# Giving each weight load of the front to the ring slot whose chunk the plan uses up first

## The reference

```
mod = silu(c) @ w_ada + b_ada                      # 2048 x 12288: shift, scale, gate, twice
h = rmsnorm(x, g_mix) * (1 + sc1) + sh1
proj = h @ w_in                                    # 2048 x 5136, columns split among three heads:
#   A: Mamba-2 SSD (conv, silu, chunked scan)   B: HGRN2 (gated recurrence)   C: S5 (diagonal scan)
x = x + gt1 * (concat(out_a, out_b, out_c) @ w_out)
h = rmsnorm(x, g_ffn) * (1 + sc2) + sh2
x = x + gt2 * hmoe(h)                              # 32 experts of width 256, top 2 inside the top group
y = rmsnorm(x, g_final)                            # and the new states are returned
```

## Time and profile before

| | |
|---|---|
| median of 3 runs | 1537.83 us (1534.4 to 1539.6) |
| the profiled execution | 1539.11 us |
| its span in the profile | 1537.4 us |
| granted TensorE clock, mean | 0.889 of 2.4 GHz |
| TensorE matmul busy | 1242.3 us (81%) |
| VectorE busy | 516.8 us (34%) |
| ScalarE busy | 197.2 us (13%) |
| GpSimd busy | 269.1 us (18%) |
| DMA | 387.06 MB, mean 252 GB/s |

### The profile page before, as it was taken

The page is one execution under the profiler, slowest core; times in us unless marked ns, Lnnn a source line. Parts: engine busy times, 40 slices in busy tenths (PEclk is TensorE's granted clock), DMA queues, the critical chain, the costliest instruction groups (busy, mean ns, idle before and its releaser), DMA issues.

```text
span 1537.4 us, 14850 instructions
## 1 busy us (share of the span) xinstructions
PE 1242.3 (81%) x5948; PEld 683.2 (44%) x5948; DVE 516.8 (34%) x1014; ACT 197.2 (13%) x319; POOL 269.1 (18%) x580
## 2 busy tenths in 40 slices
PE   5899999998979797989979785877888786878625
PEld 2456556454546464656557472332333332333214
DVE  2412657544752862245531331211112111111044
ACT  1311111101201310231210220000000000000011
POOL 3170388870000000021120002010000010000010
PEclk9899999999998898889989866999899998899856
DMA  9998468765663636352122503999999999999441
GB/s 343 363 364 299 166 216 277 268 225 177 215 222 110 219 110 219 125 150 84 55 69 110 218 31 103 421 421 419 413 413 404 404 394 413 400 412 409 203 137 69
DMA packets 140342, 387.06 MB, mean 252 GB/s; under 512 B 15435, under 2 KB 54757, under 8 KB 112814
## 3 DMA queue, kind: packets, MB, share of 16 engines
q1 hardware_dynamic: 132208, 361.91, 62.4%
q0 software_dynamic: 6784, 18.76, 3.5%
q10 hardware_dynamic: 1280, 5.42, 1.0%
HBM read 385.97 MB, written 23.15 MB: 266 GB/s over the span
## 4 chain that ended last, share of the span: by engine, by line
PE 47%; DMA 26%; DVE 10%; POOL 10%; issue 3%; ACT 2%; SPq 1%; DVEq 0%; POOLq 0%; ACTq 0%
DMA slot<-in_w_exp_up 20%; PE psum L1402 10%; PE psum L1069 9%; PE psum L1102 5%; PE psum L1347 5%; PE psum L998 3%; PE psum L959 2%; DMA slot<-in_w_ada 2%; PE psum L968 2%; POOL mem L529 2%; POOL mem L532 2%; POOL sq L527 2%; POOL sq L530 2%; PE psum L1357 1%; POOL sq L528 1%
## 5 line engine op out<-in xcount | busy, mean ns | idle before, releaser
L1402 PE MATMUL psum<-slot,mem 128*64 128x512 f32 x1024 | 259.8, 667 | 83.6 <-DMA slot<-in_w_exp_up 82.7
L1069 PE MATMUL psum<-hT,slot 128*128 128x320 f32 (+1 forms) x1056 | 309.7, 454 | 19.8 <-DMA slot<-in_w_in 19.8
L1069 PEld LDWEIGHTS psum<-hT,slot 128*128 128x128 f32 (+1 forms) x1056 | 205.8, 198 | 120.5 <-issue 28.7
L1402 PEld LDWEIGHTS psum<-slot,mem 128*64 128x64 f32 x1024 | 86.0, 154 | 255.9 <-issue 170.8
L2110 DVE TENSOR_TENSOR sq<-sq,psum 128x256 f32<-128x256 f32 x16 | 6.8, 422 | 381.7 <-ACT sq L914 381.7
L1426 PE MATMUL psum<-mem,sq 128*64 128x512 f32 x512 | 113.4, 595 | 8.6 <-issue 7.1
L968 PE MATMUL psum<-slot,cT 128*8 128x512 f32 (+1 forms) x768 | 101.9, 639 | 16.9 <-DMA slot<-in_w_ada 16.9
L613 POOL DMA_INDIRECT moe_output<-mem,idx x16 | 15.9, 995 | 485.1 <-ACT mem L918 461.5
L1102 PE MATMUL psum<-mem,slot 128*128 128x320 f32 x256 | 78.5, 467 | 0.0
L1347 PE MATMUL psum<-mem,slot 128*128 128x320 f32 x256 | 72.2, 447 | 5.4 <-DVE mem L1945 5.4
L1426 PEld LDWEIGHTS psum<-mem,sq 128*64 128x64 f32 x512 | 42.0, 137 | 69.8 <-issue 67.9
(11 more groups left out here) (422 smaller groups left out, 1323.4 us busy)
## 6 DMA issues: line engine op xcount, KB each, us to landing
slot<-in_w_ada SPq DMA_DIRECT2D x48, 2048.0 KB, 13.7
slot<-in_w_exp_gate SPq DMA_DIRECT2D x64, 1024.0 KB, 13.4
slot<-in_w_exp_up SPq DMA_DIRECT2D x64, 1024.0 KB, 16.6
mem<-in_w_exp_down SPq DMA_DIRECT2D x32, 2048.0 KB, 18.2
slot<-in_w_in SPq DMA_DIRECT2D x17, 2048.0 KB, 17.3
slot<-in_w_out SPq DMA_DIRECT2D x8, 2048.0 KB, 9.0
mem<-in_w_in SPq DMA_DIRECT2D x2, 2048.0 KB, 17.9
mem<-in_x_prompt ACTq DMA_DIRECT2D x1, 2048.0 KB, 12.0
```

The costliest lines, as they stand in the source:

```text
L1069: last = mm(psum[0:wd, grp % 2, 0:T], w[:, k, q * P:q * P + wd], hT[:, k, :], start=(k == 0), stop=(k == KD - 1))
L1402: last = mm(psum[rows_, 0, :].rearrange("p (w n) -> p w n", w=2), xe[i % 2][:, k, rows_], gate_up[h][:, :, k, :], start=(k == 0), stop=(k ...
```

## The change

A new function, `give_slots`, walks through the chunks at build time. It keeps for each buffer the count at which it becomes free, and gives the next chunk to the buffer with the lowest count. `ring_slot`, `landing` (the value of the buffer's landing semaphore that TensorE waits for) and `slot_free` (the count that SP waits for) read the result. The chunks, their order in SP's queue, the plan's order and the number and sizes of all transfers and instructions stay as they are.

```diff
 EARLY_BANK = (4, 5, 6, 7, 1, 3)
-SLOT = (1, 2, 0, 3)
-LANDED = {0: 6, 1: 5, 2: 5, 3: 3}
+FIRST_LANDED = {0: 6, 1: 5, 2: 5, 3: 3}
+FIRST_FREE = {1: 14, 2: 15, 0: 16, 3: 22}
...
+def give_slots():
+
+    free, landed, places = dict(FIRST_FREE), dict(FIRST_LANDED), []
+    for n in range(len(CHUNKS) + 4):
+        s = min(free, key=lambda x: free[x])
+        landed[s] += 1
+        places.append((s, free[s], 16 * landed[s]))
+        free[s] = DONE[n] if n < len(CHUNKS) else work_ + n
+    return places
+
+
+PLACES = give_slots()
...
         def ring_slot(n):
-            return SLOT[n % RING]
+            return PLACES[n][0]
 
         def landing(n):
-            return 16 * (LANDED[ring_slot(n)] + n // RING + 1)
+            return PLACES[n][2]
 
         def slot_free(n):
 
-            return (14, 15, 16, 22)[n] if n < RING else DONE[n - RING]
+            return PLACES[n][1]
```

## The result

The change makes the kernel faster: 1521.55 us in the median of 5 runs (1515.35 to 1523.61) against 1537.8 us (1534.4 to 1539.6), a ratio of 0.9888 with a 95% interval of 0.9868 to 0.9907. That is 17.2 us by the ratio (14.3 to 20.3) and 16.3 by the medians; 19.7 were forecast. The profiled execution took 1521.55 us, its span is 1519.8 us, 17.6 less than before.

A forecast was written before the change was run, and what follows sets the result against it. TensorE was taken to wait for expert weights (82.7 us, unchanged) and, in the front, `w_in` loads (19.8 us, three waits). 8.4 + 0 + 10.1 + 1.2 = 19.7 us gave a forecast median of 1518.1 us, range 1511 to 1526.

The forecast's parts named there:

- What each load gains, and that it lands in time: 19 of 57 loads wait for fewer pieces; chunks 33 and 45 land 6.8 and 6.4 us before they are wanted.
- rival of late landings: `w_in` loads land too late and more than a third of the gain is lost; chance 0.05.
- Place one: TensorE's wait before 445.24 us, chunk 33, piece 67: 6.84 us of wait plus 1.57 of slow piece, gain 8.4 us.
- moves along whole: At place one, the 4.14 us wait for VectorE before L1187 shifts earlier with the scores, its length unchanged.
- Place two: TensorE's wait before 518.84 us, chunk 39, piece 76: wait for VectorE grows from 6.07 to 14.1 us, gain nothing.
- rival of three full waits: TensorE holds VectorE's chain at place two, so 8.0 us more come, 1510.1 us; chance 0.07.
- one chain of their own: At place two, VectorE and ScalarE run from 497.32 us without waiting for TensorE.
- Slower: Place two's 14.1 us wait leaves the clock at half for long, adding 28.6 us, 1546.7 us; chance 0.02.
- Place three: TensorE's wait before 586.01 us, chunk 45, piece 84: 7.24 us wait and slow piece go, gain 10.1 us.
- Only the waits go, the clock stays low: Pieces at places one and three stay at 10.45 and 11.73 us; gain 15.3 us, 1522.5 us; chance 0.12.
- The store: VectorE's 5.93 us wait at L1873 shortens by 1.2 us (bounds 0 and 1.9), with TensorE's 661.6 as floor.
- Everything else nothing: Outside the three places and the store, the other moved loads and buffer order cost nothing.

The follow-up runs named there:

- e5: The kernel before, except that chunks 33 and 45 alone take the buffer that is free first; 1518.13 us, ratio 0.9894.
- e11: e10 with the convolution of chunk 15 held until level one of the second pass is done; 1510.38 us, ratio 0.983.
- e2: The kernel before, except that chunk 39 alone takes the buffer that is free first; 1536.8 us, ratio 1.0006.
- e7: The full change, with the SSD step sizes moved from before the second HGRN2 pass to before its output step; 1521.12 us, ratio 0.9891.
- e8: The kernel before, with the same move of the SSD step sizes as e7; 1532.36 us, ratio 0.9971.
- e10: e7 with hg_prep of the second pass ahead of the copies in ScalarE's order; 1506.2 us, ratio 0.9805.
- e4: The full change's buffers, but each load issued at the count of the kernel before; 1537.91 us, ratio 1.0006.
- e3: The kernel before, except that chunk 45 alone takes the buffer that is free first; 1531.06 us, ratio 0.9963.

## Why the prediction was right, and where it was off

- **What each load gains, and that it lands in time: right.** In-pieces 67, 76 and 84 started without idle time. The median landing of a `w_in` load fell from 17.3 us to 11.9. The rival of late landings is out.
- **Place one, 8.4 us: right at the place, 8.4.** The pieces behind it gave 3.0 back, a term that the sum didn't have. I had said that the 4.14 us wait "moves along whole". It does, but the two in-pieces after it take 10.47 + 10.12 us, where the one after that wait took 9.61 and the next 8.88 in the kernel before. In seven of the nine profiles without place one's wait B to C is 35.4 us or more; in e5 and e11 it is 33.3, the value of all five profiles with the wait. The record shows what else sets e5 and e11 apart: an in-piece some 40 us ahead of place one, after a wait of 3.1 us that all kernels have, took 8.88 us there and 10.57 in the other twelve profiles. First the full change, then e5:

```profile
399.45 10.57 PE L1083 MATMUL psum<-hT,slot 128*128 128x320 f32 x32
```

```profile
402.48 8.88 PE L1085 MATMUL psum<-hT,slot 128*128 128x320 f32 x32
```

  This is also why A to B is 1.7 us shorter in these two. So the 3.0 us aren't the price of the removed wait alone: in these profiles they stand only where both came together, the wait removed and the slow piece ahead of it. Why isn't shown.
- **Place two, nothing: right.** The rival of three full waits falls by e2. That a chain of VectorE and ScalarE holds the place is shown by e7, e8 and e10, which shorten it from 43.0 to 31.8 us in two steps. I had described it as "one chain of their own", with "no wait for TensorE after 497.32"; in full the chain has a second way in, ScalarE's copy of piece 74, hidden behind the step sizes until e7. The rival *Slower* is out too: after the wait of 13.31 us the in-piece took 10.09 us, less than the 10.73 after 6.07.
- **Place three, 10.1 us: 10.8 in its stretch**, 0.6 of it because the piece before it at D took 10.09 in place of 10.73 us. My 10.1 came from one profile; by e2 and e4 the same wait and piece are worth some 8.0. By e3 alone the time gives only 5.7 us (3.2 to 8.0). Why it is less than the stretch isn't settled: only one of e3's 9 executions was profiled, and that was one of its faster, 1525.75 us.
- **Only the waits go, the clock stays low: wrong at the places, where both pieces took 8.88 us**, and close to right in sum (15.3 us against 16.3 measured), since low clock came back elsewhere.
- **The store, 1.2 us: wrong.** The mechanism is there, 5.0 us to landing against 2.1. No gain shows: TensorE's products, which I had put at "661.6" and took as a fixed floor, came 3 us later against L1232 on a lower clock, and F to G is 2.0 us longer. VectorE's wait was 5.97 us, where I had said 4 to 5. The rule of the Trainium skill cited for it ("DMA: Bandwidth & Descriptors", queues, rings and completion order), alternation packet by packet, would also give nothing for the store, but by a store that hardly stands behind a load. One that lands 3 us later beside a second load speaks against its use here.
- **Everything else nothing: right, as far as the intervals reach.** e4 and e5 show nothing for the buffers and for the other 17 loads, within the few us that their intervals leave. "Up to 380 us TensorE never waits for a load" holds from 148 us on; the waits for `w_ada` before that are the ones the chain names, and the change doesn't touch them.
- **The size.** 19.7 us were forecast; 16.3 were measured by the medians and 17.2 (14.3 to 20.3) by the ratio, so by the times alone the forecast isn't off. In the two profiles the two places make 18.5 forecast and 19.2 found, and what is missing is the clock behind them and the store. That the total came so close is in part luck: place three came out above what e2 and e4 would give, and slow pieces behind place one took from it.

## What to carry to other kernels

Where buffers come free out of turn, let a queue that works strictly in order wait for the buffer that is free first; what it gives is read from the few waits that the old turn makes, here two of 19 earlier loads. Before a wait is counted as gain, look at the next wait on the same engine and at the chain that ends it: a wait of 5.7 us plus its slow matmuls was worth nothing under a chain of another engine and 6.7 us of its stretch once the chain was short. And shorten that chain by moving work that isn't due yet, looking at each engine's own order: here one move alone gave nothing on top of the ring's change, two together gave 13 us.

## What the runs showed of the hardware that was not expected

The same work on TensorE takes several microseconds more or less, by where the clock is low. The page's view of stretches shows it around the store (from:to, length, busy us, then clock, DMA share, GB/s), first before, then after:

```profile
652.00:664.00 12.00, 7.46 (x52) 5.54 (x51) 3.81 (x8) 8.87 (x8) 6.73 (x9) 0.98 0.95 301
```

```profile
634.00:646.00 12.00, 9.95 (x41) 6.84 (x42) 3.36 (x7) 7.66 (x8) 4.89 (x8) 0.72 0.83 219
```

The first out piece there takes 4.47 us at 0.98 and 6.33 at 0.72. With the same instructions in the same order, the five executions of the changed kernel spread over 8 us, and the mean clock goes with them: 1515.35 and 1515.64 us at 0.895, 1521.55 at 0.892, 1522.64 and 1523.61 at 0.889 and 0.890. In other kernels it goes with them less or not at all: e3 took 1529.99 us at 0.896 and 1523.68 at 0.891. The last column of the table differs by up to 5.3 us between kernels whose expert stages are the same; in e3 TensorE is busy there for 432.98 us at 0.89, before for 439.72 at 0.87, with as many matmuls. So in a kernel with many short waits of TensorE, which matmuls run at 1.2 GHz changes from one execution to the next, and single profiles differ in this by nearly as much as a removed wait is worth; a removed wait seems to change it too (B to C), but the profiles don't separate the two. What sets it isn't shown here.
